# Weight layout, the order of the DRAM sums, the gate seam's orders and half-size accumulating transfers in a one-core encoder block

## The chip, the cores and the metric

The kernel runs on one core of a Trainium2 chip. The time is the device time of one execution in microseconds; the number shown for a kernel is the median of its runs. The core has five engines with queues of their own: TensorE (PE, matmuls), VectorE (DVE), ScalarE (ACT), GpSimd (POOL) and SyncE (SP, which only issues transfers). The transfers of all of them run on the same 16 DMA engines. "Transfers of GpSimd" below are those that GpSimd issues; only they can add to their target.

## The reference

One layer on 512 tokens of width 2048, float32:

```python
xn = rms_norm(h, norm_mix_g)
proj = xn @ w_in                                   # q, k, v of two mixers
att_a = chunk_band_attention(..., A_PREV_CHUNKS, bias_a, a_sinks)   # window 128, 16 heads
att_b = chunk_band_attention(..., B_PREV_CHUNKS, rel_pos_bias(b_rel_bias), None)
y_a, y_b = att_a @ w_branch_a, att_b @ w_branch_b
gates = sigmoid(xn @ w_gate)
merged = gates[..., :D] * y_a + gates[..., D:] * y_b
h = h + merged @ w_out
hn = rms_norm(h, norm_mlp_g)
h = h + square(relu(hn @ w_mlp_in)) @ w_mlp_out    # 2048 -> 8192 -> 2048
out = rms_norm(h, norm_final_g)
```

## The kernel before

Every product is made of three matmuls: each float32 operand is split by ScalarE into a high part (rounded to `float32r`, a copy) and by VectorE into a low part (the difference), and PE adds high x high, low x high and high x low in PSUM.

The stages follow each other in time:

1. **w_in with attention** (0 to about 597 us). The weights come in 88 *units* of 128 x 1024 elements, four to a block of 256 output columns. `load` (line 587) puts a unit into one of four landing slots, when the unit four before it has been split; `split` on ScalarE and VectorE makes `w_hi` and `w_lo` (two slots each); PE uses it and counts `unit_used`. Between the units PE, ScalarE and VectorE do the 32 heads. Two of the eight columns of the gates are computed here too.
2. **Branch products** (to 774.8 us): 32 more units of w_branch_a and w_branch_b, so `unit_used` reaches 120.
3. **Gate products** (48 *gate units*, counted by `gate_used`). Here, and in the up and down products, the product of 2 x 2 blocks is made with seven block products instead of eight. For this, *forms* are needed: sums and differences of the blocks. For the gate weights VectorE makes them in `gate_sums` (lines 1496 to 1506) from four blocks that a load brings; for x it makes them in `x_form_block`, `x_form_sums` and `x_form_low`, in three batches; ScalarE makes the high parts in `x_form_high` and `gate_high`. `keep_branch` on ScalarE takes finished branch products out of PSUM; those of mixer b go to DRAM through two staging buffers (`store_yb` on SP) and come back later (`load_yb`).
4. **w_out** (32 units, `unit_used` up to 152), eight blocks in the order `OUT_BLOCKS`. After each block VectorE adds the residual. GpSimd makes the forms of the new hidden state in `form_sums` (line 1919), as soon as eight half blocks are there; ScalarE makes their high parts in `form_high`, in line between its `split`s.
5. **Up product** (128 units), **down product** (16 steps of 14 pieces), final norm.

The forms of the down weights, and those of the first and last eight up units, are not made in SBUF but in DRAM, by GpSimd's transfers: `totals` (line 1940) runs over 18 *sets*. A set has four blocks b0 to b3 of 1 MB and four sums: s0 = b0 + b1, s1 = b1 + b2, s2 = s0 + b2, s3 = s2 + b3. Each sum is a copy into the place of the sum and then an accumulating transfer onto it. `totals_copied` and `totals_added` count them, 16 for each transfer. The loop at line 1974 opens set m by a gate on `unit_used` or `gate_used`, and after the last set come `form_sums` on the same queue.

What sets the order around the change are the instruction queues of the engines, written out by hand: an instruction that waits holds up all behind it on its engine. On SP the stores `store_yb`, the loads of x forms and the gate loads are in one line (lines 688 to 709). On VectorE and ScalarE the loops over the gate units (lines 1581 and 1043 on) hold the x forms of the third batch between `gate_low` and `gate_high` of the early units.

`in_w_in`, `in_w_gate`, `in_w_branch_a`, `in_w_branch_b` and `in_w_out` lie in DRAM as matrices of rows of 256-column slices, so a unit comes in runs of 1 KB, four to a partition.

## Time and profile before

| | |
|---|---|
| median of 3 runs | 2498.41 us (2495.18 to 2500.89) |
| profiled execution, its own time | 2498.66 us |
| its span, first to last instruction | 2496.8 us |
| PE busy | 2449.5 us, 98% |
| VectorE, ScalarE, GpSimd busy | 1814.9, 1119.1, 200.7 us |
| mean granted TensorE clock | 0.995 |
| moved by DMA | 527.87 MB, mean 211 GB/s |
| DMA packets | 240981, of them 139808 under 2 KB |

The kernel is read from one profiled execution. The page gives busy time per engine, the chain of work that ended last, and the costliest groups of instructions; the trace behind it is asked for waits, for a timeline of one engine, and for windows. Times in the rows are from the span's start. DMA-issuing instructions do not count as busy, so GpSimd's 200.7 us say nothing of how long its queue is occupied: its timeline does. "issue" as a releaser means that the engine waited for nothing that the profile shows.

### The profile page before, as it was taken

The page shows a single profiled execution, that of the slowest core. Times are in us where ns is not written, and L with a number is a line of the kernel's source. Part 1 is how long each engine was busy: PE and PEld are TensorE (multiplying, and loading weights), DVE is VectorE, ACT ScalarE, POOL GpSimd, SP SyncE. Part 2 cuts the span into 40 slices and gives each one's busy share as a digit, 9 for nine tenths or more (in the row PEclk, how much of TensorE's full clock was granted, in tenths as well). Part 3 has the DMA queues.
Part 4 walks back from the last instruction along what each step waited for, and adds up shares of the span by engine and source line. Part 5 has one row for each costly group of instructions (what it writes and reads, how often), then busy time and mean ns, then how long its engine had stood idle before and what let it go on. Part 6 is the DMA issues. An engine that isn't in the chain of part 4 may idle for free.

```text
span 2496.8 us, 36310 instructions
## 1 busy us (share of the span) xinstructions
PE 2449.5 (98%) x15026; PEld 2205.5 (88%) x15026; DVE 1814.9 (73%) x2488; ACT 1119.1 (45%) x1414; POOL 200.7 (8%) x185
## 2 busy tenths in 40 slices
PE   9999999999998999999999999999999999999998
PEld 8898898898887999888799999999998888888886
DVE  6566565556546888733698888888869888877898
ACT  5566655556333333421433443333335444444445
POOL 0010100001000000001300000000001011110010
PEclk9999999999999999999999999999999999999999
DMA  7789888888998988999564344444468666566653
GB/s 259 191 233 232 227 230 232 218 237 230 263 260 233 247 249 248 267 267 277 158 205 151 127 135 128 127 136 135 130 229 333 231 226 218 195 227 234 229 194 110
DMA packets 240981, 527.87 MB, mean 211 GB/s; under 512 B 31120, under 2 KB 139808, under 8 KB 239664
## 3 DMA queue, kind: packets, MB, share of 16 engines
q1 hardware_dynamic: 201360, 374.01, 45.2%
q0 software_dynamic: 39168, 151.00, 25.4%
q8 instruction: 118, 1.93, 0.3%
q10 hardware_dynamic: 288, 0.54, 0.1%
q14 instruction: 47, 0.39, 0.0%
HBM read 497.14 MB, written 179.35 MB: 271 GB/s over the span
## 4 chain that ended last, share of the span: by engine, by line
PE 51%; DMA 29%; issue 14%; DVE 3%; POOL 2%; SPq 0%; ACT 0%; ACTq 0%; POOLq 0%; DVEq 0%
DMA down_totals<-in_down_blocks 17%; PE bank L2017 17%; PE bank L2018 17%; PE bank L2019 17%; DMA down_totals<-down_totals 8%; DMA up_totals<-in_up_ends 2%; POOL down_totals L1952 1%; DMA up_totals<-up_totals 1%; DVE ring L1805 0%; DVE up_lo L1697 0%; DMA stream<-in_x_features 0%; POOL down_totals L1949 0%; DVE form_lo_b L1663 0%; POOL form_raw_a L1924 0%; DVE stream L1833 0%
## 5 line engine op out<-in xcount | busy, mean ns | idle before, releaser
L1105 ACT ACTIVATE up_hi<-up_raw 128x1792 fp32r<-128x1792 f32 x128 | 218.1, 1704 | 402.3 <-PE bank L2019 392.1
L1154 ACT ACTIVATE ring<-down_raw 128x1024 fp32r<-128x1024 f32 x224 | 237.5, 1061 | 312.4 <-PE bank L2019 312.4
L1231 DVE TENSOR_TENSOR w_lo<-landing,w_hi 128x1024 fp32r<-128x1024 f32 x150 | 184.7, 1232 | 259.8 <-ACT w_hi L835 259.7
L1805 DVE TENSOR_TENSOR ring<-down_raw,ring 128x1024 fp32r<-128x1024 f32 x224 | 285.1, 1282 | 67.6 <-ACT ring L1154 67.6
L835 ACT ACTIVATE w_hi<-landing 128x1024 fp32r<-128x1024 f32 x150 | 158.8, 1059 | 366.5 <-PE bank L2019 359.3
L2017 PE MATMUL bank<-xn_hi,w_hi 128*128 128x512 f32 x792 | 313.4, 396 | 9.4 <-DVE w_lo L1231 7.2
L1697 DVE TENSOR_TENSOR up_lo<-up_raw,up_hi 128x1792 fp32r<-128x1792 f32 x128 | 259.8, 2030 | 84.0 <-ACT up_hi L1105 84.0
L2019 PE MATMUL bank<-xn_hi,w_lo 128*128 128x512 f32 x792 | 309.6, 391 | 0.0
L2018 PE MATMUL bank<-xn_lo,w_hi 128*128 128x512 f32 x792 | 309.2, 390 | 0.0
L2017 PE MATMUL bank<-ring,down_forms 128*128 128x512 f32 x656 | 255.5, 390 | 0.9 <-DVE ring L1805 0.9
L2018 PE MATMUL bank<-ring,down_forms 128*128 128x512 f32 x656 | 255.2, 389 | 0.0
L2019 PE MATMUL bank<-ring,down_forms 128*128 128x512 f32 x656 | 255.2, 389 | 0.0
L2017 PE MATMUL bank<-form_hi_b,up_hi 128*128 128x256 f32 x896 | 253.8, 283 | 0.4 <-DVE up_lo L1697 0.4
L2017 PE MATMUL bank<-form_hi_a,up_hi 128*128 128x256 f32 x896 | 253.6, 283 | 0.1
L2019 PE MATMUL bank<-form_hi_a,up_lo 128*128 128x256 f32 x896 | 253.6, 283 | 0.0
L2018 PE MATMUL bank<-form_lo_b,up_hi 128*128 128x256 f32 x896 | 253.6, 283 | 0.0
L2019 PE MATMUL bank<-form_hi_b,up_lo 128*128 128x256 f32 x896 | 253.6, 283 | 0.0
L2018 PE MATMUL bank<-form_lo_a,up_hi 128*128 128x256 f32 x896 | 253.6, 283 | 0.0
L2017 PEld LDWEIGHTS bank<-xn_hi,w_hi 128*128 128x128 f32 x792 | 149.4, 189 | 40.1 <-DVE w_lo L1231 6.5
L2019 PEld LDWEIGHTS bank<-xn_hi,w_lo 128*128 128x128 f32 x792 | 149.2, 188 | 32.0
L2018 PEld LDWEIGHTS bank<-xn_lo,w_hi 128*128 128x128 f32 x792 | 149.5, 189 | 29.8 <-issue 0.2
L2017 PEld LDWEIGHTS bank<-form_hi_b,up_hi 128*128 128x128 f32 x896 | 172.0, 192 | 0.7 <-DVE up_lo L1697 0.6
(263 smaller groups left out, 5712.3 us busy)
## 6 DMA issues: line engine op xcount, KB each, us to landing
down_totals<-in_down_blocks POOLq DMA_DIRECT2D x96, 1024.0 KB, 9.5
up_raw<-in_up_units SPq DMA_DIRECT2D x128, 512.0 KB, 3.6
down_raw<-down_totals SPq DMA_DIRECT2D x128, 512.0 KB, 4.6
down_raw<-in_down_blocks SPq DMA_DIRECT2D x96, 512.0 KB, 4.6
landing<-in_w_in SPq DMA_DIRECT2D x71, 512.0 KB, 6.6
down_totals<-down_totals POOLq DMA_DIRECT2D x32, 1024.0 KB, 6.2
gate_raw<-in_gate_units SPq DMA_DIRECT2D x48, 512.0 KB, 5.9
landing<-in_w_out SPq DMA_DIRECT2D x32, 512.0 KB, 7.2
```

The costliest lines, as they stand in the source:

```text
L835: nc.scalar.activation(hi, landing[:, u % LAND, :], ACT.Copy).then_inc(unit_hi, 1)
L1105: nc.scalar.activation(up_hi[n % 2], up_raw[n % 3][:, 1:8, :], ACT.Copy).then_inc(up_hi_done, 1)
L1154: nc.scalar.activation(ring[i % RING][:, 0, :], raw_of(i), ACT.Copy).then_inc(piece_hi, 1)
L1231: nc.vector.tensor_tensor(lo, landing[:, u % LAND, :], hi.bitcast(F32), ALU.subtract).then_inc(unit_lo, 1)
L1697: nc.vector.tensor_tensor(up_lo[n % 2], up_raw[n % 3][:, 1:8, :], up_hi[n % 2].bitcast(F32), ALU.subtract).then_inc(up_lo_done, 1)
L1805: nc.vector.tensor_tensor(part[:, 1, :], raw_of(i), part[:, 0, :].bitcast(F32), ALU.subtract)\
L1952: pool.dma_start(dst, src, accum_op=ALU.add, max_dma_last_dim=4096).then_inc(totals_added, 16)
L2017: nc.tensor.matmul(dst, a_hi, b_hi, start=start, stop=False, **kw)
L2018: nc.tensor.matmul(dst, a_hi, b_lo, start=False, stop=False, **kw)
L2019: return nc.tensor.matmul(dst, a_lo, b_hi, start=False, stop=stop, **kw)
```

## The change

- **Weights.** `w_in`, `w_branch_a`, `w_branch_b`, `w_gate` and `w_out` are laid out in DRAM so that a unit is one piece of 4 KB per partition. `load` takes it whole. The first 1 KB per partition of the first unit is still loaded ahead of the rest.
- **DRAM sums.** In place of `totals`, `totals_round(i)` for i from 0 to 20: copy all four blocks of set i; then, after the copies of the sets before i, add b1 and b2 for set i - 1; then, after all additions of earlier rounds, add s0 to s2 for set i - 2, and s2 to s3 for set i - 3. The number of copies and additions and what they sum is as before. The gates of the rounds are 8 + 8i units used for i under 14, then 3, 18 and 33 gate units, then units 122, 126, 130 and 133.
- **Halves.** Each accumulating transfer of 1 MB becomes two of 512 KB, one for 64 partitions each, and its packets 2048 bytes instead of 4096. Copies keep 4096.
- **The seam's orders.** SP: `store_yb(5)` goes ahead of the loads of gate units 1 and 2. VectorE: the third batch's `x_form_block`s and sums go from behind `gate_low(1)` to behind `gate_low(2)`, and `x_form_low` 6 and 7 from behind 3 and 4 to both behind 4. ScalarE: `x_form_high` 6 and 7 from behind `gate_high` 2 and 3 to behind 3 and 4.

```diff
-            def load(b, u, src, width):
+            def load(b, u, src):
 
                 s = u % LAND
                 if not (isinstance(b, int) and b == 0):
                     sp.wait_ge(unit_lo, 4 * b + (u - LAND + 1))
-                dst = landing[:, s, :].rearrange("p (k n) -> p k n", n=width)
-                sp.dma_start(dst, src).then_inc(unit_landed[s], 16)
-
-            def load_block(b, w, col, units=4):
...
             for w in range(BRANCH_UNITS):
-                src, nb = (wba, wbb)[w // 16], w % 16 // 2
-                load(B2 + w // 4, w % 4, src[:, KU * (w % 2):KU * (w % 2 + 1), nb * CB:(nb + 1) * CB], CB)
+                src, nb = (w_branch_a, w_branch_b)[w // 16], w % 16 // 2
...
+            store_yb(5)
             load_gate(1)
             load_gate(2)
             load_x_forms(2)
             for n in range(3, GATE_UNITS):
                 load_gate(n)
-                if n in (3, 4, 5):
+                if n in (4, 5):
                     store_yb(n + 2)
...
-                        sp.wait_ge(totals_added, 16 * 4 * (end + 1))
+                        sp.wait_ge(totals_added, 32 * added_by(end + 3))
...
-            sp.wait_ge(totals_added, 16 * 4 * (2 + STEPS))
+            sp.wait_ge(totals_added, 32 * 4 * (2 + STEPS))
...
                 gate_high(n)
                 if n == 1:
                     keep_branch(15)
-                elif n in (2, 3):
-                    x_form_high(n + 4)
+                elif n in (3, 4):
+                    x_form_high(n + 3)
...
                 gate_low(n)
-                if n == 1:
+                if n == 2:
                     x_form_block(6)
                     x_form_block(7)
                     x_form_sums(2)
-                elif n in (3, 4):
-                    x_form_low(n + 3)
+                elif n == 4:
+                    x_form_low(6)
+                    x_form_low(7)
                 if n >= 4 and GATE_ORDER[n - 4][1] == 3:
...
+        def added_by(i):
+
+            return 2 * min(i, SETS) + min(max(i - 1, 0), SETS) + max(i - 2, 0)
...
-            def totals(m, part):
+            def totals_of(m):
 
                 if m < 2:
-                    blocks, sums = up_ends[m], up_totals[m]
-                else:
-                    step = m - 2
-                    blocks, sums = down_blocks[step // 2, step % 2], down_totals[step // 2, step % 2]
-
-                def copied(src, dst):
-                    pool.dma_start(dst, src, max_dma_last_dim=4096).then_inc(totals_copied, 16)
-
-                def added(src, dst):
-                    pool.dma_start(dst, src, accum_op=ALU.add, max_dma_last_dim=4096).then_inc(totals_added, 16)
-
-                if part == 0:
-                    copied(blocks[0], sums[0])
-                    copied(blocks[1], sums[1])
-                elif part == 1:
-                    pool.wait_ge(totals_copied, 16 * (4 * m + 2))
+                    return up_ends[m], up_totals[m]
+                return down_blocks[(m - 2) // 2, m % 2], down_totals[(m - 2) // 2, m % 2]
+
+            def copied(src, dst):
+                pool.dma_start(dst, src, max_dma_last_dim=4096).then_inc(totals_copied, 16)
+
+            def added(src, dst):
+
+                for h in (slice(0, P // 2), slice(P // 2, P)):
+                    pool.dma_start(dst[h], src[h], accum_op=ALU.add, max_dma_last_dim=2048).then_inc(totals_added, 16)
+
+            def totals_round(i):
+
+                if i < SETS:
+                    blocks, sums = totals_of(i)
+                    for f in range(4):
+                        copied(blocks[f], sums[f])
+                if 1 <= i <= SETS:
+                    pool.wait_ge(totals_copied, 16 * 4 * i)
+                    blocks, sums = totals_of(i - 1)
                     added(blocks[1], sums[0])
                     added(blocks[2], sums[1])
-                elif part == 2:
-                    pool.wait_ge(totals_added, 16 * (4 * m + 2))
-                    copied(sums[0], sums[2])
-                elif part == 3:
-                    pool.wait_ge(totals_copied, 16 * (4 * m + 3))
-                    added(blocks[2], sums[2])
-                elif part == 4:
-                    pool.wait_ge(totals_added, 16 * (4 * m + 3))
-                    copied(sums[2], sums[3])
+                if 2 <= i <= SETS + 1:
+                    pool.wait_ge(totals_added, 32 * added_by(i - 1))
+                    sums = totals_of(i - 2)[1]
+                    added(sums[0], sums[2])
+                if 3 <= i:
+                    sums = totals_of(i - 3)[1]
+                    added(sums[2], sums[3])
+
+            for i in range(SETS + 3):
+                if i < 14:
+                    pool.wait_ge(unit_used, 8 + 8 * i)
+                elif i < 17:
+                    pool.wait_ge(gate_used, (3, 18, 33)[i - 14])
                 else:
-                    pool.wait_ge(totals_copied, 16 * (4 * m + 4))
-                    added(blocks[3], sums[3])
-
-            for m in range(2 + STEPS):
-                if m < 13:
-                    pool.wait_ge(unit_used, 12 + 8 * m if m < 10 else 84 + 10 * (m - 9))
-                else:
-                    pool.wait_ge(gate_used, (4, 14, 25, 36, 47)[m - 13])
-                for part in range(6):
-                    totals(m, part)
+                    pool.wait_ge(unit_used, UNITS1 + BRANCH_UNITS + (2, 6, 10, 13)[i - 17])
+                totals_round(i)
...
+    def units(w):
+        columns = w.shape[-1] // CB
+        return w.reshape(-1, KU, P, columns, CB).transpose(3, 0, 2, 1, 4).reshape(columns, -1, P, KU * CB)
```

## Rows read from the trace of the kernel before

**Rows 1.** The page, part 1: busy us (share of the span) xinstructions of each engine.

```profile
PE 2449.5 (98%) x15026; PEld 2205.5 (88%) x15026; DVE 1814.9 (73%) x2488; ACT 1119.1 (45%) x1414; POOL 200.7 (8%) x185
```

**Rows 2.** Waits of PE: engine, line, waited for: total us, times, longest us.

```profile
PE bank L2017 <- DVE gate_lo L1511: 20.5, 12, 9.4
PE bank L2017 <- DVE w_lo L1231: 9.0, 4, 6.1
```

**Rows 3.** Windows: stretch, length, busy us per engine, clock, DMA share, GB/s.

```profile
775.00:800.00 25.00, 15.63 (x120) 15.43 (x119) 16.27 (x19) 9.07 (x6) 2.04 (x3) 0.80 0.87 254
1175.00:1200.00 25.00, 18.94 (x81) 15.35 (x80) 7.74 (x9) 7.30 (x6) 11.31 (x7) 0.93 0.76 204
```

**Rows 4.** Timeline around 1195 us: start, length, engine, line, instruction [idle before <-releaser].

```profile
1194.38 1.70 ACT L1082 ACTIVATE form_hi_a<-form_raw_a 128x1792 fp32r<-128x1792 f32 x1 [11.82 <-POOL form_raw_a L1921]
...
1197.06 1.23 DVE L1231 TENSOR_TENSOR w_lo<-landing,w_hi 128x1024 fp32r<-128x1024 f32 x1 [12.03 <-ACT w_hi L835]
...
1198.34 0.80 PE L2017 MATMUL bank<-xn_hi,w_hi 128*128 128x512 f32 x1 [6.06 <-DVE w_lo L1231]
```

**Rows 5.** Timeline of GpSimd (POOL): first, one set of sums, last.

```profile
77.48 1.32 POOL L1949 DMA_DIRECT2D up_totals<-in_up_ends  x2 [77.03 <-PE bank L2019]
...
250.22 0.89 POOL L1952 DMA_DIRECT2D down_totals<-in_down_blocks  x1 [6.25 <-DMA down_totals<-down_totals]
250.78 0.89 POOL L1949 DMA_DIRECT2D down_totals<-in_down_blocks  x1
258.90 0.57 POOL L1949 DMA_DIRECT2D down_totals<-in_down_blocks  x1 [7.23 <-issue]
266.28 0.92 POOL L1952 DMA_DIRECT2D down_totals<-in_down_blocks  x1 [6.80 <-DMA down_totals<-in_down_blocks]
275.33 0.91 POOL L1952 DMA_DIRECT2D down_totals<-in_down_blocks  x1 [8.13 <-issue]
...
1183.85 0.89 POOL L1952 DMA_DIRECT2D down_totals<-in_down_blocks  x1 [7.78 <-DMA down_totals<-down_totals]
1184.53 7.41 POOL L1924 TENSOR_TENSOR form_raw_a<-form_raw_a 128x1024 f32<-128x1024 f32 x3
```

**Rows 6.** The page, part 4: chain that ended last, DMA and code lines.

```profile
DMA down_totals<-in_down_blocks 17%; PE bank L2017 17%; PE bank L2018 17%; PE bank L2019 17%; DMA down_totals<-down_totals 8%; DMA up_totals<-in_up_ends 2%; POOL down_totals L1952 1%; DMA up_totals<-up_totals 1%; DVE ring L1805 0%; DVE up_lo L1697 0%; DMA stream<-in_x_features 0%; POOL down_totals L1949 0%; DVE form_lo_b L1663 0%; POOL form_raw_a L1924 0%; DVE stream L1833 0%
```

**Rows 7.** Waits of GpSimd that the profile names issue: total us, times, longest us.

```profile
POOL down_totals L1952 <- issue: 147.5, 16, 10.8
POOL down_totals L1949 <- issue: 141.1, 16, 10.5
```

**Rows 8.** Issue to landing of additions, copies, weight units, gate units; last, GpSimd's queue.

```profile
DMA to landing us min/median/max: 8.3/9.5/11.6
...
DMA to landing us min/median/max: 4.9/7.5/14.4
...
DMA to landing us min/median/max: 2.7/6.6/15.1
...
DMA to landing us min/median/max: 3.3/5.9/11.6
...
q0 software_dynamic: 39168, 151.00, 25.4%
```

**Rows 9.** Timeline of ScalarE: splits that wait for unit 32 and 122.

```profile
210.04 1.06 ACT L835 ACTIVATE w_hi<-landing 128x1024 fp32r<-128x1024 f32 x1 [1.62 <-PE bank L2019]
...
1057.21 1.05 ACT L835 ACTIVATE w_hi<-landing 128x1024 fp32r<-128x1024 f32 x1
```

**Rows 10.** Timeline at the seam, four engines: SP, ACT, DVE, PE.

```profile
778.19 0.43 SPq L667 DMA_DIRECT2D yb_rows<-gate_mix  x1
...
785.48 2.74 DVE L1471 SCALAR_TENSOR_TENSOR x_raw_c<-x_raw_c,gains,rms_row 128x512 f32<-128x512 f32 x4 [6.68 <-DMA x_raw_c<-in_x_features]
...
789.54 1.02 ACT L1003 ACTIVATE gate_mix<-bank 128x1024 f32<-128x1024 f32 x1 [12.79 <-DMA yb_rows<-gate_mix]
...
794.38 0.58 PE L2017 MATMUL bank<-x_hi_a,gate_hi 128*128 128x256 f32 x1 [9.37 <-DVE gate_lo L1511]
```

More of the change, by code:

```diff
@@ L178, in build @@
     out_tiles = out[0].rearrange("(t p) d -> p t d", p=P)
-    def rows(w):
-        return w[0].rearrange("(k p) n -> p k n", p=P)
-    win, wga, wba, wbb = rows(w_in), rows(w_gate), rows(w_branch_a), rows(w_branch_b)
-    wout = rows(w_out)
     with ExitStack() as ctx:
@@ L543, in build @@
         B4 = B3 + 8
+        SETS = 2 + STEPS
+        def added_by(i):
+            return 2 * min(i, SETS) + min(max(i - 1, 0), SETS) + max(i - 2, 0)
         N_BLOCKS1 = len(BLOCKS)
@@ L590, in load @@
                     sp.wait_ge(unit_lo, 4 * b + (u - LAND + 1))
-                dst = landing[:, s, :].rearrange("p (k n) -> p k n", n=width)
-                sp.dma_start(dst, src).then_inc(unit_landed[s], 16)
-            def load_block(b, w, col, units=4):
-                for u in range(units):
-                    load(b, u, w[:, KU * u:KU * (u + 1), bass.ds(col, CB)], CB)
+                sp.dma_start(landing[:, s, :], src).then_inc(unit_landed[s], 16)
             def strip(h):
@@ L613, in _ @@
             load_x(0, 1, x_start_landed)
-            first_col = COL0["k", "a"]
-            sp.dma_start(landing[:, 0, 0:CB], win[:, 0, first_col:first_col + CB]).then_inc(start_landed, 16)
+            first = w_in[COL0["k", "a"] // CB, 0]
+            sp.dma_start(landing[:, 0, 0:CB], first[:, 0:CB]).then_inc(start_landed, 16)
             load_x(1, 2, x_second_landed)
@@ L619, in _ @@
                 if kind == "g":
-                    w, col = wga, (0 if mixer == "a" else D) + i * CB
+                    w, column = w_gate, (0 if mixer == "a" else D // CB) + i
                 else:
-                    w, col = win, COL0[kind, mixer] + i * CB
+                    w, column = w_in, COL0[kind, mixer] // CB + i
                 for u in range(KU):
                     if n == 0:
-                        sp.dma_start(landing[:, 0, CB:].rearrange("p (k n) -> p k n", n=CB), w[:, 1:KU, col:col + CB])\
-                            .then_inc(unit_landed[0], 16)
+                        sp.dma_start(landing[:, 0, CB:], first[:, CB:]).then_inc(unit_landed[0], 16)
                     else:
-                        load(c, u, w[:, KU * u:KU * (u + 1), col:col + CB], CB)
+                        load(c, u, w[column, u])
                     if c == 0 and u == 0:
@@ L688, in _ @@
             for w in range(BRANCH_UNITS):
-                src, nb = (wba, wbb)[w // 16], w % 16 // 2
-                load(B2 + w // 4, w % 4, src[:, KU * (w % 2):KU * (w % 2 + 1), nb * CB:(nb + 1) * CB], CB)
+                src, nb = (w_branch_a, w_branch_b)[w // 16], w % 16 // 2
+                load(B2 + w // 4, w % 4, src[nb, w % 2])
                 if w == 6:
@@ L723, in _ @@
                         sp.wait_ge(gate_lo_done, GATE_UNITS - 1 + u // 2)
-                    load(B3 + n, u, wout[:, KU * u:KU * (u + 1), c * CB:(c + 1) * CB], CB)
+                    load(B3 + n, u, w_out[c, u])
                     if u == 1:
@@ L2329 @@
     others = {"x_features": inputs["x"][0].T, "norm_gains": norm_gains, "identity": np.eye(P, dtype=np.float32), "alibi": alibi_strips(),
-              "up_units": up_units, "x_turned": x_turned, "w_out": w_out, "up_ends": up_ends, "down_blocks": down_blocks, "gate_units": gate_units}
+              "up_units": up_units, "x_turned": x_turned, "w_in": units(inputs["w_in"]), "w_branch_a": units(inputs["w_branch_a"]),
+              "w_branch_b": units(inputs["w_branch_b"]), "w_gate": units(inputs["w_gate"]), "w_out": units(w_out),
+              "up_ends": up_ends, "down_blocks": down_blocks, "gate_units": gate_units}
     for name in [*_INS, *(name for name in others if name not in _INS)]:
```

## The prediction

> **What bounds the kernel now.** I read the page's busy times first: TensorE (PE) is busy 2449.5 us, 98% of the 2496.8 us span, so at most 47 us of it can be won [rows 1]. Then the waits of PE: two names carry nearly all of them, `gate_lo` with 20.5 us in 12 waits and `w_lo` with 9.0 us in 4 [rows 2]. The windows show where: the seam between the branch products and the gate products (15.6 us busy of 25, clock 0.80), and the end of the w_out stage (18.9 of 25) [rows 3]. A list of waits names only the engine that came last, so I read the second place backwards. PE sat idle for 6.06 us until 1198.34, behind a `w_lo` of VectorE, behind ScalarE, which had waited 11.82 us for GpSimd's `form_raw_a` sums [rows 4]. GpSimd issued its last DRAM addition at 1183.85 and began these sums at 1184.53, the moment it was free [rows 5].
>
> So the chain of work is the thing to read: 17% and 8% of the span are DMAs into `down_totals` [rows 6]. From 77.48 to 1184.53 the path that sets the end is not PE but GpSimd's queue of DRAM sums: 18 sets in 1107 us, 61.5 us a set, and none of the gates but the first one (on PE, 77.0 us) ever held it [rows 5, 7]. After that, 1312 us of kernel follow that the change does not touch. **The time after is therefore 2498.66 plus the move of that 1184.53**, as long as the new value is later than PE can use it (PE restarted 13.8 us after it; without its 6.06 us idle it would have wanted the sums started by 1178.5). All sums below are against the profiled execution, 2498.66 us, which lies 0.25 us over the median of the runs shown.
>
> **The queue of sums, step by step.** One set in the rows [rows 5]: an addition (250.22) and a copy behind it (250.78) go out together; the second copy leaves only at 258.90; the first addition waits for the copies (266.28); the second waits 8.13 us on "issue" (275.33), although no semaphore stands between the two in the code. "Issue" takes 147.5 + 141.1 us in 32 such places [rows 7]. So copy + copy fit in flight together, addition + copy too, but addition + addition do not, nor addition + two copies. Counting a copy as 1 (it reads 1 MB) and an addition as 2 (it reads source and target), the limit lies at 3 and under 4. Is it packets or bytes? In the change a half addition moves half the bytes in packets half as long, so it reads as many packets as a whole one did. No row tells the two apart; I take packets, since addition + addition and addition + copy write the same 2 MB and only the number of packets read differs, and keep bytes as a rival. The Trainium skill (DMA: Bandwidth & Descriptors, section SWDGE vs HWDGE vs iDMA) has GpSimd write a descriptor pair per piece into rings of limited room, which speaks for packets too.
>
> Durations. Whole addition, issue to landing 8.3 / 9.5 / 11.6 us; copy 4.9 / 7.5 / 14.4 (the long ones queued behind an addition) [rows 8]. The queue's packets took 25.4% of the span [rows 8], 634 us for 72 copies and 72 additions; at 1 to 2 by bytes read that is 2.9 us of engine work for a copy and 5.9 for an addition. The shortest ones agree: 8.3 - 4.9 = 3.4. The rest, about 3.6 us of a 9.5 us addition, is start, drain and the load queue's share, and belongs to each transfer whatever its size.
>
> The change, per edit:
> - **Copies ahead.** The four copies of a set no longer wait for anything of their own set. By the limit three go together, the fourth behind them: 4 x 2.9 + 2 (4.9 - 2.9, one drain) = 14 us instead of the 61.5 - 4 x 9.7 = 22.7 that four cost inside the old chain. Bounds: 11.8 (no drain) to 19.6 (four shortest ones, one after another).
> - **Halves.** Half an addition is 9.5 - 2.9 = 6.6 us, plus 0.2 until the next is issued: 6.8. Bounds: 4.9 (half of 9.7, nothing fixed) to 7.5 (the median copy, which reads as many bytes). I take 6.8, nearer to the copy's row since the bytes read are equal. Eight of them per round, one after another, since two do not fit: 54.4 us, less 1.5 for the first, issued while the last copy runs. The old four whole additions cost 4 x 9.7 = 38.8 (9.5 and 0.2 to the next). So this edit costs 15.6 us a set, and the copies give back 8.7 and the hidden start 1.5. **A round is 14 + 54.4 - 1.5 = 67 us.**
> - **Order in rounds.** Rounds 0, 1 and 2 hold less than a full one (4, 8 and 10 transfers) and are held by their gates (8, 16, 24 units used), so GpSimd idles early on. Round 3 opens at unit 32, 210.04 us, read from ScalarE's split that waits for that unit [rows 9]. From there 54 us per 8 units is less than 67, so no gate binds again. Rounds 3 to 17 are full: 210 + 15 x 67 = 1215. Rounds 18 to 20 hold 8 + 4 + 2 halves; PE, and so the load queue, stands still for most of it, so I take 6.1 (between 8.3 - 2.9 = 5.4 and 6.8): 86 us. The sums start at 1301 instead of 1184.5: **+116.5 us.**
> - **Waits added** stand on GpSimd alone (`totals_copied`, `totals_added` of earlier rounds); behind them is queued only the next round, and last `form_sums`. Those of rounds 1 to 17 are met when reached. SP's own waits on the sums (first `up_raw`) come after 1200 and are met.
> - **Weights in one piece.** 151 loads of 512 KB go from 1 KB runs to 4 KB. Landing was 2.7 / 6.6 / 15.1 us; `gate_raw`, same bytes in 4 KB runs in the same traffic, 3.3 / 5.9 / 11.6 [rows 8]. So 0.7 us per load on loads that PE waited for only 4 times: 0 to 3 us, hidden by the four landing slots. Lost if the cover goes: nothing here.
> - **The seam.** `keep_branch(15)` on ScalarE waited 12.79 us for a `yb_rows` store that SP had issued at 778.19 behind two loads, and `gate_high(2)` is queued behind it; VectorE's `x_raw_c` block waited 6.68 us with `gate_low(2)` behind it; PE lost 9.37 us [rows 10]. `store_yb(5)` now stands before two gate loads; ScalarE has made its copy by then (unit 116 is used, PE is at 118), so on SP it delays them by 0.5 us, and the sums that need them come 10 us later. The `x_raw_c` block goes behind `gate_low(2)`. What is late next is `gate_sums(3)`, ahead of `gate_low(2)` on VectorE: its load goes out at 777.5 and lands about 6 us later, so the stall falls to 1 to 5 us. `x_form_low` 6 and 7 both stand behind `gate_low(4)` now: 2 us more on VectorE before unit 5, 0 to 2 us lost. Net 4 to 8 us gained, 0 in the end while GpSimd sets it.
>
> Sum: 2498.66 + 116.5 = **2615**. Its own range: with 6.2 us a half, rounds of 62 and an end at 1218, 2533; with 7.5 a half, 72.5 and 1393, 2707.
>
> **A rule against, and its price.** The skill (same page, Rules for kernel authors) advises against splitting a transfer by partitions and wants one transfer over all 128. Its section on the anatomy of a GpSimd DMA gives about 2.0 us fixed plus bytes over 436 GB/s. By that figure, an estimate, a split costs 2.0 us and a half is (9.7 + 2.0) / 2 = 5.9. The rows show more fixed time (3.6), so I stay with 6.8.
>
> **Rivals.**
> - *A small fixed part.* If a half takes 5.9, a round is 60 and the end 210 + 15 x 60 + 14 x 5.4 = 1186: no change, 2500. For it: the shortest copy. Against: the medians. This is also the turning point between slower and faster.
> - *The queue keeps pace* (faster). Below about 5.2 us a half, rounds fit into the 54 us of 8 units and gates set them: round 17 opens at unit 122, 1057.21 [rows 9], and with 4.9 us a half the sums start at 1057 + 52 + 14 x 4.9 = 1178, when PE wants them; both move up by what the seam gains. Then the 6.1 us stall and about 2 us of low clock around it (0.93 over 25 us) go, the seam's 4 to 8, and some 3 of the small gate waits: 2480. For it: half the bytes could be half the time (4.9), or two halves fit in flight if the limit is bytes, or the packets are not cut. Against: 32 "issue" waits that follow the count.
> - *Contention worse*: load packets of 4 KB take a longer turn between the sum's packets. With 7.5 a half, 2707; inside the forecast's range.
>
> **How the numbers follow.** Forecast (2533 to 2707) 0.64; a bit slower still between 2504 and 2533, 0.05; small fixed part 0.06 within 0.2% (about what a measurement of this kernel can tell from no change); queue keeps pace or nearly 0.25, centred on 2480. Range: 2478 to 2690 leaves out half of the last case and the upper tail. Faster 0.25, same 0.06, slower 0.69.
>
> **What would show it.** GpSimd's timeline: half to half 6.8 us with "issue" before each (two issued 1 us apart would refute it); rounds 67 us apart; `form_raw_a` sums starting at 1301; PE idle some 110 us on `w_lo` near 1190. The seam's stall under 5 us. The sum is wrong if a half takes under 5.9.

## The result, and the profile after

The changed kernel takes 2660.91 us (median of 4 runs, 2651.09 to 2666.94), the kernel before 2498.43: a ratio of 1.0648 (95% interval 1.0627 to 1.0668), slower by about 162 us. Its profiled execution is the fastest of the four, 2651.09 us; all sums below are against that one and the 2498.66 us of before, so +152.4.

The page of the changed kernel, part 1 and part 4, beside [rows 1] and [rows 6]:

```profile
PE 2449.7 (92%) x15026; PEld 2207.0 (83%) x15026; DVE 1815.5 (69%) x2488; ACT 1118.7 (42%) x1414; POOL 263.9 (10%) x257
...
PE 54%; issue 33%; POOL 6%; DMA 4%; DVE 2%; ACT 0%; SPq 0%; ACTq 0%; POOLq 0%; DVEq 0%
```

PE has the same work (2449.7 us busy against 2449.5). A third of the chain that ended last is now "issue": GpSimd waiting for nothing that the profile shows. The waits of PE and GpSimd (total us, times, longest), beside [rows 2] and [rows 7]:

```profile
PE bank L2012 <- DVE w_lo L1225: 174.7, 4, 171.4
PE bank L2012 <- DVE gate_lo L1505: 8.4, 8, 2.6
...
POOL down_totals L1947 <- issue: 610.1, 97, 14.8
POOL down_totals L1942 <- issue: 245.5, 31, 12.5
```

One stall of 171.4 us holds the whole loss: it was 6.06 before [rows 4], and the gate waits fell by 12.1 us (20.5 to 8.4). 171.4 - 6.1 - 12.1 = 153.2, against the +152.4. The windows beside [rows 3] (length, busy us per engine, clock, DMA share, GB/s):

```profile
775.00:800.00 25.00, 20.48 (x152) 19.91 (x151) 17.02 (x22) 10.90 (x7) 2.39 (x3) 0.93 0.88 277
1175.00:1350.00 175.00, 4.71 (x21) 3.57 (x19) 0.19 (x1) 2.86 (x3) 35.72 (x35) 0.52 0.57 105
```

The seam is better filled than before (20.5 us of 25 against 15.6). Then, from 1180 to the restart (1347 to 1351), PE, VectorE and ScalarE do nothing, the granted clock of 0.52 is nearly all at its lower level of 1.2 GHz, and even the DMA engines are busy only 57% of the time. What all wait for is in GpSimd's timeline: round 8 of the sums in full, the first half of round 18, and the end; then the restart on three engines, as in [rows 4, 5].

```profile
553.83 0.91 POOL L1942 DMA_DIRECT2D down_totals<-in_down_blocks  x1
559.57 1.11 POOL L1942 DMA_DIRECT2D down_totals<-in_down_blocks  x2 [4.82 <-issue]
572.08 0.55 POOL L1942 DMA_DIRECT2D down_totals<-in_down_blocks  x1 [11.39 <-issue]
572.62 0.93 POOL L1947 DMA_DIRECT2D down_totals<-in_down_blocks  x1
581.56 0.91 POOL L1947 DMA_DIRECT2D down_totals<-in_down_blocks  x1 [8.01 <-issue]
590.02 0.88 POOL L1947 DMA_DIRECT2D down_totals<-in_down_blocks  x1 [7.56 <-issue]
598.22 0.89 POOL L1947 DMA_DIRECT2D down_totals<-in_down_blocks  x1 [7.31 <-issue]
604.18 0.88 POOL L1947 DMA_DIRECT2D down_totals<-down_totals  x1 [5.07 <-DMA down_totals<-in_down_blocks]
609.61 0.89 POOL L1947 DMA_DIRECT2D down_totals<-down_totals  x1 [4.55 <-issue]
615.31 0.88 POOL L1947 DMA_DIRECT2D down_totals<-down_totals  x1 [4.81 <-issue]
624.25 0.90 POOL L1947 DMA_DIRECT2D down_totals<-down_totals  x1 [8.06 <-issue]
624.81 0.92 POOL L1942 DMA_DIRECT2D down_totals<-in_down_blocks  x1
...
1261.93 0.89 POOL L1947 DMA_DIRECT2D down_totals<-in_down_blocks  x1 [4.78 <-issue]
...
1336.76 0.90 POOL L1947 DMA_DIRECT2D down_totals<-down_totals  x1 [4.81 <-issue]
1337.42 7.26 POOL L1919 TENSOR_TENSOR form_raw_a<-form_raw_a 128x1024 f32<-128x1024 f32 x3
...
1347.14 1.70 ACT L1076 ACTIVATE form_hi_a<-form_raw_a 128x1792 fp32r<-128x1792 f32 x1 [177.15 <-POOL form_raw_a L1916]
...
1351.09 0.79 PE L2012 MATMUL bank<-xn_hi,w_hi 128*128 128x512 f32 x1 [171.38 <-DVE w_lo L1225]
```

L1942 are the copies, L1947 the halves. No two halves are in flight together: each leaves only when the one before has landed, and mostly the profile shows nothing that it waits for ("issue"). Full rounds open at 211.10, 272.24, ... 1198.91, so rounds 4 to 16 take 926.7 / 13 = 71.3 us each. The sums in SBUF start at 1337.42, 152.9 us after the 1184.53 of [rows 5], and the time grew by 152.4.

### The profile page after: what moved, and what is told of

Same layout as the page of the kernel before. It is cut to its first block, busy times and chain, and to the rows that moved or that the text cites. A ratio compares the mean times of both kernels' runs of the same rounds, so it can differ in the third digit from the quotient of the medians.

```text
span 2649.3 us, 36384 instructions
## 1 busy us (share of the span) xinstructions
PE 2449.7 (92%) x15026; PEld 2207.0 (83%) x15026; DVE 1815.5 (69%) x2488; ACT 1118.7 (42%) x1414; POOL 263.9 (10%) x257
## 4 chain that ended last, share of the span: by engine, by line
PE 54%; issue 33%; POOL 6%; DMA 4%; DVE 2%; ACT 0%; SPq 0%; ACTq 0%; POOLq 0%; DVEq 0%
PE bank L2012 18%; PE bank L2014 18%; PE bank L2013 18%; DMA down_totals<-in_down_blocks 4%; POOL down_totals L1947 4%; POOL down_totals L1942 1%; DVE ring L1800 0%; PE bank L2087 0%; DVE up_lo L1692 0%; DVE form_lo_b L1658 0%; POOL form_raw_a L1919 0%; PE bank L2101 0%; DVE stream L1828 0%; PE bank L2122 0%; DVE stream L1849 0%
```

## The experiments

The theory, A: the split of the additions sets the time, since two halves do not fit in flight together and each carries a fixed part. The rivals: the rounds themselves cost it, or the weight layout does; and on the limit, that it counts bytes or transfers instead of packets. Each timed run has its own runs of the kernel before on the same chip (medians 2499.23 to 2501.36), and the ratio is to these; e9 ran once and has no ratio.

### e1: whole additions

```diff
-                for h in (slice(0, P // 2), slice(P // 2, P)):
-                    pool.dma_start(dst[h], src[h], accum_op=ALU.add, max_dma_last_dim=2048).then_inc(totals_added, 16)
+                pool.dma_start(dst, src, accum_op=ALU.add, max_dma_last_dim=4096).then_inc(totals_added, 16)
```

(and 16 for 32 in the waits on `totals_added`)

> The changed kernel with only the halves undone: each addition is one transfer of 1 MB in 4096-byte packets, everything else as changed. Theory A (the split sets the time): a round is four copies, 18.6 us as measured in the changed kernel, and four additions of 9.5 to 9.7 us, so 56 to 58 us in place of 71; round 3 opens at 211 us, round 17 at about 1065 and the sums in SBUF start near 1130, before the tensor engine wants them (1178). Then the tensor engine sets the end: no stall of over 3 us at 1180, the seam's gain of some 12 us comes through, 2475 to 2482 us. Rival B (the new order of the rounds costs as much as the split, since the fourth copy waits for the three ahead of it): rounds of over 62 us, the sums start after 1200, 2510 us or more.

Measured: 2501.50 us, ratio 1.000 (0.998 to 1.002). Undoing the halves gives back all that the change lost, about 159 us. But the gain that I expected did not come. GpSimd's timeline at the end:

```profile
1062.50 1.68 POOL L1942 DMA_DIRECT2D down_totals<-in_down_blocks  x3 [44.67 <-PE bank L2013]
1078.16 0.56 POOL L1942 DMA_DIRECT2D down_totals<-in_down_blocks  x1 [13.98 <-issue]
1078.70 0.97 POOL L1946 DMA_DIRECT2D down_totals<-in_down_blocks  x1
...
1187.92 0.90 POOL L1946 DMA_DIRECT2D down_totals<-down_totals  x1 [11.04 <-PE bank L2013]
1188.59 7.34 POOL L1919 TENSOR_TENSOR form_raw_a<-form_raw_a 128x1024 f32<-128x1024 f32 x3
```

The queue keeps pace (54 to 61 us a round), then stands idle 44.7 us for the gate of round 17 (and about 33 ahead of round 16). Behind that gate are four copies and eleven additions: 16 us and ten intervals of 10.9 to the last. (The profile names PE for the wait before 1187.92, but the unit that gates round 20, at 5.44 us a unit, had been used by about 1122; the addition before it landed just ahead of 1187.92.) In my expectation I forgot round 17's own transfers. Neither A's 2475 to 2482 nor B's 2510 came true. So the pipeline's gain is given back by its gates, and the end is where the old chain had it.

### e2: halves in packets of 4096 bytes

```diff
-                    pool.dma_start(dst[h], src[h], accum_op=ALU.add, max_dma_last_dim=2048).then_inc(totals_added, 16)
+                    pool.dma_start(dst[h], src[h], accum_op=ALU.add, max_dma_last_dim=4096).then_inc(totals_added, 16)
```

> The changed kernel with one number changed: the half additions in packets of 4096 bytes instead of 2048. A half is then 128 packets of source instead of 256, with the same bytes. Theory A (the limit of what GpSimd can have in flight counts packets): two halves go out about 1 us apart, a wait on issue stands only before every second one, four whole additions cost 30 to 40 us instead of 53, rounds fall to 50 to 58 us, and the time is that of the tensor engine, 2475 to 2482 us. Rival B (it counts bytes, or transfers): halves still go one by one, 6.6 us each, rounds 71 us, 2640 to 2670 us.

Measured: 2505.53 us, ratio 1.0022 (1.0005 to 1.0038). GpSimd's timeline in a round:

```profile
392.01 1.71 POOL L1947 DMA_DIRECT2D down_totals<-in_down_blocks  x2
397.71 0.81 POOL L1947 DMA_DIRECT2D down_totals<-in_down_blocks  x1 [3.99 <-issue]
408.14 0.81 POOL L1947 DMA_DIRECT2D down_totals<-in_down_blocks  x1 [9.63 <-issue]
408.67 2.06 POOL L1947 DMA_DIRECT2D down_totals<-down_totals  x2
```

The same halves with the same bytes now go out two and three together. Bytes and number of transfers are refuted as the limit. The time misses A's 2475 to 2482 as e1's did: rounds of 53 to 60 us, the same late gates, sums at 1197.71. So the split by itself costs almost nothing behind the better order (2505.53 against 2501.50 in e1); the 159 us come from halves whose packets are halved too.

### e3: the split in the old chain

```diff
-                    pool.dma_start(dst, src, accum_op=ALU.add, max_dma_last_dim=4096).then_inc(totals_added, 16)
+                    for h in (slice(0, P // 2), slice(P // 2, P)):
+                        pool.dma_start(dst[h], src[h], accum_op=ALU.add, max_dma_last_dim=2048)\
+                            .then_inc(totals_added, 16)
```

(and 32 for 16 in the waits on `totals_added`)

> The kernel before with only the additions split into two halves of 2048-byte packets, in the old chain of sets. Theory A (a split costs two halves of 6.6 us for one addition of 9.7, whatever the order around it): 4 x 3.5 = 14 us a set, 18 sets, +252 us: 2720 to 2770 us, all of it as one stall of the tensor engine near 1190. Rival B (the loss comes from the rounds, not from the split): 2500 to 2530 us.

Measured: 2732.37 us, ratio 1.0946 (1.0893 to 1.1000). The sums in SBUF start at 1422.49, so a set takes (1422.5 - 77.5) / 18 = 74.7 us in place of 61.5: 13.2 us a set, **3.3 us for each addition split in halves of 2048-byte packets**. Rival B is out. The rounds are not the cause; they save part of what the split costs.

### e4: packets of 8192 bytes

```diff
-                pool.dma_start(dst, src, max_dma_last_dim=4096).then_inc(totals_copied, 16)
+                pool.dma_start(dst, src, max_dma_last_dim=8192).then_inc(totals_copied, 16)
...
-                pool.dma_start(dst, src, accum_op=ALU.add, max_dma_last_dim=4096).then_inc(totals_added, 16)
+                pool.dma_start(dst, src, accum_op=ALU.add, max_dma_last_dim=8192).then_inc(totals_added, 16)
```

(against e1; also, the wait for the additions of earlier rounds stands ahead of the two additions from the blocks)

> As the kernel with whole additions, but copies and additions in packets of 8192 bytes (one per partition), and the wait for the additions of earlier rounds moved ahead of the two additions from the blocks. Theory A (packets in flight are the limit): each transfer counts half, copies no longer wait for each other except by their own length, the four leave within 5 us, two additions go 1 us apart; rounds are then shorter than the 54 us between their gates, the gates set them, and the time is 2475 to 2482 us as with whole additions. Rival B (bytes or transfers are the limit): the timeline of GpSimd looks as with 4096-byte packets. Rival C: packets twice as long hold up the weight loads, landing of a unit rises from 4.9 to over 6.5 us and the tensor engine waits more, over 2485 us.

Measured: 2522.46 us, ratio 1.0094 (1.0062 to 1.0125). GpSimd's timeline:

```profile
376.07 2.08 POOL L1942 DMA_DIRECT2D down_totals<-in_down_blocks  x4 [20.86 <-PE bank L2014]
378.14 0.87 POOL L1946 DMA_DIRECT2D down_totals<-in_down_blocks  x1
392.49 0.83 POOL L1946 DMA_DIRECT2D down_totals<-in_down_blocks  x1 [13.48 <-issue]
```

Four copies and an addition go out together. One count fits all four kernels: copies of 4096-byte packets count 1, of 8192 a half; additions 2 when whole at 4096, 2 as a half at 2048, 1 as a half at 4096, 1 when whole at 8192; and never more than 3 are in flight. The 2 of an addition is fitted, as if both its sources counted: the trace lists 256 packets for it as for a copy. The sums start at 1175.59, before PE wants them. Yet it is slower, not A's 2475 to 2482, and rival C says where: the landing of a `w_in` unit is 9.0 us against 6.3 in e1, and PE, busy 173.2 us of the 175 from 600 to 775 us in e1, is busy 163.7 of them here.

### e5: whole additions, late gates earlier

```diff
-                    pool.wait_ge(gate_used, (3, 18, 33)[i - 14])
-                else:
-                    pool.wait_ge(unit_used, UNITS1 + BRANCH_UNITS + (2, 6, 10, 13)[i - 17])
+                    pool.wait_ge(gate_used, (3, 15, 26)[i - 14])
+                elif i == 17:
+                    pool.wait_ge(gate_used, 37)
```

> The kernel with whole additions, with the gates of the late rounds moved ahead: rounds 15, 16 and 17 at gate units 15, 26 and 37 (before 18, 33 and unit 122), rounds 18 to 20 without a gate. With the old gates GpSimd stood idle 34 us ahead of round 16 and 45 us ahead of round 17 and the sums in SBUF started at 1188.6 us. Theory A (the late gates and the four rounds behind them set the 1188.6): the sums start between 1110 and 1140 us, the tensor engine's last stall on w_lo of 4.4 us goes with the low clock around it, 2493 to 2497 us. Rival B (the gates kept transfers out of the gate stage, and that is worth more): gate_lo waits rise above 25 us, 2501 us or more.

Measured: 2495.87 us, ratio 0.9967 (0.9948 to 0.9986): faster than before. GpSimd is free 31.7 us before its sums can start (1150.17, now behind VectorE, and so later than A's 1110 to 1140). The gate waits stay at 20.8 us. A.

### e6: halves only at the gate stage

The diff adds to e5 that in rounds 13 to 15 an addition is two halves of 2048-byte packets:

```diff
+                if i in HALVED:
+                    for h in (slice(0, P // 2), slice(P // 2, P)):
+                        pool.dma_start(dst[h], src[h], accum_op=ALU.add, max_dma_last_dim=2048)\
+                            .then_inc(totals_added, 16)
+                else:
+                    pool.dma_start(dst, src, accum_op=ALU.add, max_dma_last_dim=4096).then_inc(totals_added, 16)
```

> As the kernel with whole additions and early gates, but the additions of rounds 13, 14 and 15 (about 770 to 980 us, the gate stage) in halves of 2048-byte packets. Theory A (one half in flight at a time leaves the DMA engines more to the loads, which is what shortened the tensor engine's waits in the gate stage from 18 us to 8): the waits on gate_lo fall from 21 to 8 to 12 us, w_out starts at 1040 to 1047 us in place of 1056, the sums start by 1165 us and the tensor engine does not wait for them, 2481 to 2488 us. Rival B (the shorter waits of the changed kernel come from its queue being late, so that its rounds met other work, or from chance): gate_lo stays at 17 us or more, 2493 us or more.

Measured: 2489.41 us, ratio 0.9945 (0.9919 to 0.9971). The waits of PE:

```profile
PE bank L2019 <- DVE gate_lo L1508: 13.3, 8, 6.5
PE bank L2019 <- DVE w_lo L1228: 6.4, 4, 3.0
```

The gate waits fell by a third to 13.3, just over A's bound of 12; w_out starts at 1042.4 us, the sums at 1162.22. The time lies just above A's 2481 to 2488 and below B's. The halves that lose 159 us as a rule of the whole queue seem to gain some microseconds where the queue has time to spare: the median lies 6.5 us below that of e5, from which only the halves differ, but the intervals of the two ratios overlap, so how much they gain is not shown.

### e7 and e8: the seam's orders alone, the weight layout alone

Both on the kernel before. e7 is the hunks around `store_yb`, `x_form_high` and `x_form_block`, with these at its core:

```diff
+            store_yb(5)
...
-                if n == 1:
+                if n == 2:
                     x_form_block(6)
```

e8 is `load`, its callers and `units`:

```diff
-                dst = landing[:, s, :].rearrange("p (k n) -> p k n", n=width)
-                sp.dma_start(dst, src).then_inc(unit_landed[s], 16)
+                sp.dma_start(landing[:, s, :], src).then_inc(unit_landed[s], 16)
```

> The kernel before with only the seam's orders of the change. Theory A (GpSimd's queue of sums sets the end): the sums in SBUF start at 1184 to 1188 us as before, the wait of 9.4 us at the seam falls to 2 to 5, the stall on w_lo near 1190 grows by the same amount, 2496 to 2503 us. Rival B (the seam's wait fell for want of DMA traffic, not by the orders): the wait at 780 to 795 us stays above 7 us, the time is the same too.

Measured: 2497.36 us, ratio 0.9985 (0.9962 to 1.0008), no difference that this can tell. The seam's wait is 4.20 us in place of 9.37 (A). In this execution the queue of sums came to its end at 1167.21, outside A's 1184 to 1188: 17 us before that of [rows 5] with the same instructions on GpSimd. Nor did the stall on `w_lo` grow (4.7 us in all, 9.0 before). PE gained nearly nothing from the earlier end (2497.04 us against 2498.66), which fits the forecast's reading that PE wants the sums no earlier than about 1178.

> The kernel before with only the weight units in one piece per partition. Theory A (packets of 4 KB shorten a landing little, and the landing slots hide it): the median landing of a w_in unit goes from 6.6 us to 6.0 to 6.4, the rounds of sums stay 61.5 us a set, the sums start at 1180 to 1188, 2494 to 2502 us. Rival B (the layout alone brought the 4.9 us of the changed kernel): landing 4.9 to 5.3 us, the sets of the sums take under 60 us, the sums start before 1170 and the time falls to 2490 or less. Rival C (load packets of 4 KB hold up the sums' packets): sets of over 63 us, over 2515 us.

Measured: 2511.85 us, ratio 1.0042 (1.0015 to 1.0070): slower, between A and C. The landing of a `w_in` unit is 5.6 us (before 6.6), so the loads do become faster; but a set takes 61.9 us, the sums start at 1191.60, and the wait at the seam is 11.56 us. In the profiled execution, 2504.95 us, the late sums account for all of its +6.3; but e7 shows that this start moves by 17 us from one execution to another, so that the layout made them late is not shown, and why the median lies 7 us higher still, the trace does not show either.

### e9: an addition by itself

```diff
-                    pool.wait_ge(unit_used, UNITS1 + BRANCH_UNITS + (2, 6, 10, 13)[i - 17])
+                    pool.wait_ge(unit_used, UNITS1 + BRANCH_UNITS + (17, 17, 17, 17)[i - 17])
```

> The kernel with whole additions, with the gates of rounds 17 to 20 moved back to unit 137 used, so that the last additions run while the tensor engine and with it the load queue stand still; nothing else differs. It measures an addition of 1 MB by itself, from the issue of one to the issue of the next; in the changed kernel a half under the same conditions takes 5.6 us. With a fixed part f per transfer and half the rest for half the bytes, the whole takes 11.2 - f. Theory A (f is the 3.6 us of the prediction): 7.6 us. Rival B (f is 2.0 us): 9.2 us. Rival C (nothing fixed): 11 us. The sums in SBUF start about 1150 + 15 + 40 + 7 such additions, 1258 to 1282 us, and the time is 2498.7 plus their distance to 1184.5, 2572 to 2597 us.

Measured: 2556.16 us, a single execution. The diff is against e1. GpSimd's timeline, from where SP has nothing more to load:

```profile
1192.48 0.90 POOL L1946 DMA_DIRECT2D down_totals<-in_down_blocks  x1 [7.36 <-issue]
1201.34 0.88 POOL L1946 DMA_DIRECT2D down_totals<-in_down_blocks  x1 [7.96 <-issue]
1210.06 0.90 POOL L1946 DMA_DIRECT2D down_totals<-down_totals  x1 [7.84 <-DMA down_totals<-in_down_blocks]
...
1242.22 0.90 POOL L1946 DMA_DIRECT2D down_totals<-down_totals  x1 [7.16 <-issue]
1242.89 7.26 POOL L1919 TENSOR_TENSOR form_raw_a<-form_raw_a 128x1024 f32<-128x1024 f32 x3
```

Six intervals in 49.7 us: 8.3 us a whole addition. Halves under the same conditions in the changed kernel (1261.93 to 1336.76, 13 intervals): 5.76. The fixed part is 2 x 5.76 - 8.3 = 3.2 us, between A and B and nearer to A, and it agrees with the 3.3 of e3. The whole ones have 4096-byte packets and the halves 2048, so the 3.2 is of both changes together; a lone half of 4096-byte packets in e2 (the last, at 1197.08) landed in 5.2 us, those of 2048 in the changed kernel in 5.0 to 6.0, which suggests that little of it is the packets'. The round opened at 1134 and not 1150, so time and start of the sums lie below the ranges given by about as much.

### e10 and e11: everything a gate earlier, halves in rounds 12 to 16, with and without the new layout

```diff
-                if i < 14:
-                    pool.wait_ge(unit_used, 8 + 8 * i)
-                elif i < 17:
-                    pool.wait_ge(gate_used, (3, 15, 26)[i - 14])
-                elif i == 17:
-                    pool.wait_ge(gate_used, 37)
+                if i < 16:
+                    pool.wait_ge(unit_used, 8 * i or 1)
+                elif i < 18:
+                    pool.wait_ge(gate_used, (12, 24)[i - 16])
```

(on e6, with `HALVED` from 12 to 16; e11 is the same with `load` and the weight arrays of before)

> As the kernel with halves at the gate stage, but with every round one gate earlier (8 i units used for round i up to 15, gate units 12 and 24 for rounds 16 and 17, none behind), and halves in rounds 12 to 16, so that they also lie over the seam. Theory A (halves under the gate loads pay as long as the queue ends before the tensor engine wants the sums): the wait at the seam falls from 6.5 to 2 to 3 us, gate_lo waits to 7 to 10 us in all, the sums start at 1130 to 1160 us, 2478 to 2487 us. Rival B (two-sided noise of the gate stage; halves had nothing to do with it): gate_lo stays at 13 us or more, 2489 us or more.

Measured: 2485.96 us, ratio 0.9953 (0.9932 to 0.9974). A for the time, just over A's 10 for the gate waits (10.2 us in all), but not for the seam, whose wait is still 6.5 us. With e6 the fastest that was found.

> As the run before it, but with the weights in DRAM as they were (four runs of 1 KB per partition). Theory A (the layout alone cost 0.4% in the old chain because its 4 KB packets hold up GpSimd's queue; off the path that sets the end it costs nothing): the same time within 0.2%, the landing of a w_in unit 0.5 to 1 us longer. Rival B (the 4 KB load packets harm the gate stage itself, by longer waits at the seam): 5 to 10 us faster than the run with the new layout.

Measured: 2490.42 us, ratio 0.9965 (0.9944 to 0.9986). The two ratios do not differ by more than their intervals; a `w_in` unit lands in 7.3 us against 6.7. A, as far as it can be told: off the path that sets the end the layout is worth nothing that can be measured.

### e12: the rounds alone

`totals_round` and its loop in place of `totals`, with the whole additions of e1, and nothing else:

```diff
-            for m in range(2 + STEPS):
+            for i in range(SETS + 3):
```

> The kernel before with only the new order of the DRAM sums: rounds with the change's gates, whole additions in 4096-byte packets, old weight layout, old seam. Theory A (rounds take 54 to 58 us, but the late gates and the 11 additions behind unit 122 give the gain back): the sums start at 1180 to 1192 us, the wait at the seam is 7 to 10 us as before, 2496 to 2505 us. Rival B (the rounds by themselves gain, and the weights or the seam lose it): the sums start before 1170, under 2492 us.

Measured: 2498.72 us, ratio 0.9992 (0.9974 to 1.0009); the sums start at 1189.20, round 17 having opened at 1064.97 after 42.9 us idle. The rounds took 50 to 66 us, more spread than the forecast 54 to 58, and the wait at the seam 10.3. A.

## Why the prediction was right, point by point

**Right: what bounds the kernel.** "The time after is 2498.66 plus the move of that 1184.53" held wherever the sums were late:

| kernel | sums start, us | moved by | time moved by |
|---|---|---|---|
| whole additions (e1) | 1188.59 | 4.1 | 3.2 |
| rounds alone (e12) | 1189.20 | 4.7 | 3.1 |
| layout alone (e8) | 1191.60 | 7.1 | 6.3 |
| halves, 4096 (e2) | 1197.71 | 13.2 | 12.6 |
| whole, late gates (e9) | 1242.89 | 58.4 | 57.5 |
| the change | 1337.42 | 152.9 | 152.4 |
| split in the old chain (e3) | 1422.49 | 238.0 | 238.2 |

**Right: halves do not overlap**, and packets are what is counted (e2, e4).

**Nearly right: the halves' term.** I had 6.8 us a half; in rounds 4 to 16 it was 7.0, from one half to the next with no copy ahead. (The 52.7 us from the first half to the next round's first copy look like the 52.9 of the forecast, but that copy leaves beside the eighth half, so they hold seven intervals and not eight.) The split costs 3.3 us an addition (e3), 13.2 a round where I had 15.6; the fixed part is 3.2 us where I had 3.6. The Trainium skill (DMA: Bandwidth & Descriptors, Anatomy of one DMA) has about 2.0 us; the measurement decides for more. The advice of the Trainium skill (DMA: Bandwidth & Descriptors, Rules for kernel authors) not to split a transfer by partitions held in this case for the queue as a whole: the halves cost 159 us (e1), and where they were in flight together they won nothing (e2).

**Wrong in size: the copies.** A round took 71.3 us in place of 67. The mean of rounds 4 to 16, from the rows of GpSimd: the second and third copy leave 6.6 us after the first, when the last half of the round before has landed; from there it is 12.0 us to the first half, 10.6 on to the second, six times 6.9 to the eighth, and 7.2 to the next round's second copy. At 7.0 a half, eight make 55.7 (54.4 in the forecast). That leaves 15.6 us for the four copies with the first half's start beside the last of them, where I had 14 - 1.5 = 12.5. So 3.1 of the 4.4 us are the copies' and 1.3 the halves'.

The step that failed is "three go together, the fourth behind them: 4 x 2.9 + 2". It lets the fourth follow without a gap. In e1 the three copies issued from 1062.50 on land 6.5, 9.1 and 14.2 us after their issue, one after another, and the fourth leaves at 1078.16, 0.35 us after the third has landed and 9 after the first. It is so in rounds 2 to 17 of both the change and e1: 0.34 to 0.35 us behind the third's landing, 6.5 to 12.1 behind the first's. The queue runs empty once more, and the fourth pays a start and an end of its own; by the forecast's 4.9 - 2.9 = 2.0 for that, the term would have been 14.5, an estimate. Why GpSimd waits for the last of the three and not for the first, no run shows. The rest may be the load queue's share of the same engines, which an average over the span does not give; that is argued and not shown.

The sum again, 1337.4 against 1301: opening 211.1 against 210 (+1.1), round 3 with 61.1 (-5.9), 13 rounds of 4.3 more (+55.7), round 17 with 63.0 (-4.0), and the tail, 14 halves in 75.5 us against 86 (-10.5: with SP still a half takes 5.76 us and not 6.1, and the sums start 0.66 us after the last is issued, without waiting for it to land). That is +36.4, and the forecast of 2615 becomes the profiled 2651; the median of 2661 lies 10 us higher. Both are inside the case's own range (2533 to 2707) and the stated one (2478 to 2690). That the miss was 36 us and not 56 is luck: the two ends erred the other way.

**Right: the seam** (9.37 to 2.55 us; alone to 4.20) **and its being hidden.** The 2.55 is one of the better executions: PE's first wait at the seam was 1.9 to 8.6 us in the ten kernels with the new orders, five of them over 5 us, and 7.6 to 11.6 in the four with the old. But of the 12 us of gate waits that went, most is not the orders' doing. PE's wait on `gate_lo`, over all executions:

| additions in the gate stage | us |
|---|---|
| whole, or halves of 4096-byte packets: before, e1, e2, e4, e5, e7, e8, e9, e12 | 20.5, 21.0, 20.3, 23.6, 20.8, 19.2, 23.5, 14.1, 24.9 |
| halves of 2048-byte packets: after, e3, e6, e10, e11 | 8.4, 10.5, 13.3, 10.2, 8.7 |

The groups do not overlap, but e9's 14.1 comes near e6's 13.3, and e9 has the same instructions in this stage as e1 with 21.0: one execution differs from another by 7 us. I had no term for this. That less is summed per microsecond is not the cause by itself. From 775 to 1040 us GpSimd's queue moved 33.6 MB in e1 and 33.2 in e2 (waits of 21.0 and 20.3), 33.7 in e6 and 33.0 in e11 (13.3 and 8.7), and least of all in e4, 27.2 MB, with 23.6. Whether it is the shorter packets or that only one half is in flight at a time stays open: the two go together in all these kernels.

**Wrong in sign: the layout.** I had 0 to 3 us gained and hidden; alone it costs 0.42% (e8). "Lost if the cover goes: nothing here" overlooked that GpSimd's queue is itself the path and shares the engines with the loads; that the cost arises there is argued, not shown (see e7 and e8). For the change's longer rounds the nearest pair is e10 and e11, rounds 12 to 16: 72.3 us a round with the new layout, 70.4 with the old, in one execution each, where single rounds differ by 8 us. Of the `w_in` landing, 6.6 before, 4.9 after, the halves alone bring 4.8 (e3) and the layout alone 5.6 (e8).

**Rivals.** The small fixed part needed a half of 5.9; it took 7.0 in full rounds. "The queue keeps pace" is what whole additions do (e1), and it gave 2501, not 2480: my 2480 rested on sums at 1178, with 9.8 us for each of the eleven additions behind the gate of round 17; they took 10.9, the gate opened 5 us later, and the sums start at 1188.6. The contention rival had the direction right, but less of it in the halves (7.0, not 7.5) than in the copies.

## What to carry to other kernels

Ask of a queue that sets the end how much of each transfer does not shrink with its size: here 3.2 of 8.3 us, and 72 splits with halved packets cost 238 us in the old chain and 159 behind the better order. Split so that the pieces can be in flight together, and it costs next to nothing (e2). A pipeline gains nothing if the gate of its last round stays where the old chain had it: count the transfers behind that gate first. And a transfer split that is wrong for the path can be right in one stage, where the queue has slack and its neighbour is the one that waits.

## What the runs showed of the hardware

- What GpSimd has in flight follows a count of packets, not bytes or transfers: with 1 for a 1 MB copy in 256 packets and 2 for an addition in as many, never more than 3. Halving the packet length with the transfer left the count and took away the overlap; the same half in 4096-byte packets restored it. But what fits in flight brought no more speed (e2: rounds of 53 to 60 us, e1: 54 to 61).
- A place that comes free is not always taken. The copies in flight land one after another (6.5, 9.1 and 14.2 us from issue, e1), but the fourth leaves 0.35 us after the third has landed, in all of rounds 2 to 17 of e1 and of the change.
- An accumulating DRAM-to-DRAM transfer took, from issue to issue, 8.3 us for 1 MB (e9) and 5.76 for 512 KB (the change) with the load queue still, 10.9 us for 1 MB under the w_out loads (e1).
- With all of GpSimd's transfers in 8192-byte packets the loads beside them land later, 9.0 us against 6.3 (`w_in` units, e4 and e1).
- The same instructions on GpSimd ended 17 us apart in two executions (1184.53 and 1167.21, e7, which differs only at the seam).
